# A gated-linear-attention stage on one Trainium2 core: decays computed during the projections, 64-token blocks, and the last pair's outputs placed inside the output projection

## What is computed

```python
y_f = _fourier_mix(z_f)                      # 256 of the 1024 output features
logg = log_sigmoid(z_g @ gate_w + gate_b) / 16
b = cumsum(logg, within a chunk)
qd, kd = q * exp(b), k * exp(-b)
att = where(mask, qd @ kd^T, 0)              # mask: lower triangle, 64 x 64
o = qd @ s + att @ v                         # s: 64 x 128 state before the chunk
s = s * exp(b_last) + (k * exp(b_last - b))^T @ v
o = o_forward + flip(o_backward)
y_g = rmsnorm(o over 128) * gla_norm * silu(z_r)
mix = concat(y_f, y_g) @ mix_w_out           # 1024 x 1024
```

## Time and profile before

| | us |
|---|---|
| median of 3 runs | 2854.75 (2853.38 to 2856.09) |
| the profiled execution | 2853.26 |
| its span in the trace | 2851.5 |
| TensorE matmul busy | 2745.1 (96%) |
| VectorE / ScalarE / GpSimd busy | 1292.9 (45%) / 1023.8 (36%) / 173.3 (6%) |
| chain that ended last | TensorE 89%, VectorE 6%, ScalarE 4% |
| mean granted clock of TensorE | 0.98 of full |

### The profile page before, as it was taken

How to read it: one execution, slowest core, us unless ns; L and a number is a source line. 1 busy time by engine, 2 the same in 40 slices (tenths; PEclk the granted TensorE clock), 3 DMA queues, 4 the chain that set the end, 5 groups by cost and what they waited for, 6 DMA issues and landing times.

```text
span 2851.5 us, 41295 instructions
## 1 busy us (share of the span) xinstructions
PE 2745.1 (96%) x18134; PEld 2420.4 (85%) x18134; DVE 1292.9 (45%) x1659; ACT 1023.8 (36%) x1291; POOL 173.3 (6%) x165
## 2 busy tenths in 40 slices
PE   7999999979999999999999889999999999988998
PEld 5877878767887787877888789999999999978998
DVE  4333334374423335332345655565555544554554
ACT  4222223332321223222233444443644444444443
POOL 0000010001000000000011000010010010133100
PEclk9999999979999999999999999999999999999999
DMA  7444344501444245444234135464445456653452
GB/s 272 145 148 151 104 156 140 185 15 61 146 163 158 96 142 177 137 148 156 77 112 133 45 105 177 161 208 154 154 142 174 158 174 186 190 130 103 134 197 84
DMA packets 398611, 406.18 MB, mean 142 GB/s; under 512 B 7264, under 2 KB 397104, under 8 KB 398432
## 3 DMA queue, kind: packets, MB, share of 16 engines
...
## 4 chain that ended last, share of the span: by engine, by line
PE 89%; DVE 6%; ACT 4%; issue 1%; DMA 0%; POOL 0%; SPq 0%; ACTq 0%; DVEq 0%; POOLq 0%
PE bank L96 88%; DVE w_lo L107 2%; ACT w_hi L103 1%; PE bank L99 1%; DVE tmp L115 1%; ACT x_hi L103 1%; DVE gla_att L107 1%; DVE gla_st L115 0%; DVE df_sc L124 0%; DVE x_lo L115 0%; ACT df_e L104 0%; ACT L103 0%; DMA ident<-in_ident 0%; POOL acc L107 0%; DVE gla_ls L118 0%
## 5 line engine op out<-in xcount | busy, mean ns | idle before, releaser
L107 DVE TENSOR_TENSOR w_lo<-w_raw,w_hi 128x2048 fp32r<-128x2048 f32 (+2 forms) x331 | 694.5, 2101 | 909.6 <-ACT w_hi L103 909.0
L96 PE MATMUL bank<-x_hi,w_hi 128*128 128x256 f32 (+1 forms) x3128 | 1031.0, 330 | 17.7 <-DVE w_lo L107 6.9
L96 PE MATMUL bank<-x_hi,w_lo 128*128 128x256 f32 (+1 forms) x3128 | 1021.2, 327 | 0.0
L96 PE MATMUL bank<-x_lo,w_hi 128*128 128x256 f32 (+1 forms) x3128 | 1016.2, 327 | 0.0
L103 ACT ACTIVATE w_hi<-w_raw 128x2048 fp32r<-128x2048 f32 (+2 forms) x331 | 578.4, 1750 | 462.9 <-PE bank L96 295.4
L96 PEld LDWEIGHTS bank<-x_hi,w_hi 128*128 128x128 f32 x3128 | 596.9, 191 | 81.5 <-issue 29.8
L96 PEld LDWEIGHTS bank<-x_hi,w_lo 128*128 128x128 f32 x3128 | 596.8, 191 | 50.1
L96 PEld LDWEIGHTS bank<-x_lo,w_hi 128*128 128x128 f32 x3128 | 594.9, 191 | 49.9 <-issue 0.7
L96 PE MATMUL bank<-hid_hi,w_hi 128*128 128x512 f32 (+1 forms) x1056 | 356.0, 337 | 1.7 <-ACT ada_rows L103 1.7
L96 PE MATMUL bank<-hid_lo,w_hi 128*128 128x512 f32 (+1 forms) x1056 | 354.9, 336 | 0.0
L96 PE MATMUL bank<-hid_hi,w_lo 128*128 128x512 f32 (+1 forms) x1056 | 354.8, 336 | 0.0
...
## 6 DMA issues: line engine op xcount, KB each, us to landing
...
```

Source lines behind the costliest of these rows:

```text
L96: return Issued(self.eng and self.eng.matmul(out, lhsT, rhs, start=start, stop=stop, skip_group_check=loose))
L107: return Issued(self.eng and self.eng.tensor_tensor(out, a, b, op))
```

## The change

Seven things change in the even mixer.

1. All decays are computed during the projections. `pe_gates` of pairs 0, 1 and 2 follow the rows units at 0, 1024 and 1280. VectorE puts their passes between the copies of the units at 1024, 1280 and 1536, ScalarE the exponentials and logarithms beside them; q, k and the results of all three pairs have places of their own, and r's places serve as scratch until SiLU fills them. The mask of the cumulative sum is loaded earlier, into the tile `diag`.
2. The products inside a block are 64 x 64 for each chunk, and the mask passes go over half as many elements.
3. The outputs come by token (128 tokens x 128 features): stationary are the masked products and the decayed queries, moving are v and the states. TensorE waits for its own inside part before it adds the part of the states.
4. The mean square is then a sum along the free axis: four activations with an accumulated sum for each head on ScalarE, a square root, a reciprocal and one multiplication on VectorE. The 24 matmuls of squares and the 24 of diagonals go; four transposes for each head (`pe_pair_turn`) turn the normed outputs into features by token.
5. Pair 0's inside work stands ahead of the Fourier mix, whose evictions move to ScalarE; its sums stay in PSUM until they are split.
6. In time, outputs of pair m follow the inside work of pair m+1.
7. The outputs and the turn of pair 2 stand inside `project_first` of the output projection, ahead of input blocks 4 and 6 (`aside`).

TensorE's side, SyncE's, ScalarE's and VectorE's (`pe_pair_turn` does four transposes for each head; `dve_gates`, `dve_decays` and `dve_decayed` keep their passes and change their places):

```diff
     for kk in range(1, KC):
+        if kk in aside:
+            aside[kk](e)
         wait_operand(e, x, kk)
         for i in range(4):
...
-    e.dma_start(Even(k).seg[:, :], k.io["segments"]).then_inc(k.load("seg"), "seg")
+    e.dma_start(t.seg, k.io["segments"]).then_inc(k.load("seg"), "seg")
 
...
     e.wait_ge(k.product, ("even", 2304, 1))
     e.dma_start(t.ft[:, :, :], k.io["fourier_time"]).then_inc(k.load("four_t"), "four_t")
+    e.dma_start(t.lim[:, :, :, :], k.io["limits"]).then_inc(k.load("lim"), "lim")
     e.dma_start(t.fd[:, :, :], k.io["fourier_dim"]).then_inc(k.load("four_d"), "four_d")
-    e.dma_start(t.lim[:, :, :, :], k.io["limits"]).then_inc(k.load("lim"), "lim")
...
     u.last = "even_g"
-    for c0, dst in ((0, "zf"), (1024, "v"), (1280, "v"), (1536, "v")):
+    for i, c0 in enumerate(EVEN_ROWS):
         u = take(e, ("even", c0), w, 0, KC, c0, 256)
         for tb in range(4):
-            bank = e.bank(("even", c0, tb), k.vector, (dst, c0, tb))
+            bank = e.bank(("even", c0, tb), k.vector, ("rows", c0, tb))
             project_rows(e, u, x, tb, bank).then_inc(k.product, ("even", c0, tb))
         u.last = ("even", c0, 3)
+        if i < 3:
+            pe_gates(e, t, i)
         pe_ada_step(e)
-    k.after(2, sp_even_segments)
-    pe_gates(e, t, 0)
     for c in range(3):
         u = take(e, ("even", 1792 + 256 * c), w, 0, KC, 1792 + 256 * c, 256)
...
+    pe_pair_inside(e, t, 0)
+    pe_fourier(e, t)
+    pe_pair_inside(e, t, 1)
+    pe_pair_outputs(e, t, 0)
+    pe_pair_inside(e, t, 2)
+    pe_pair_turn(e, t, 0)
+    pe_pair_outputs(e, t, 1)
+    pe_pair_turn(e, t, 1)
```

```diff
+    for d in range(2):
+        e.wait_ge(k.pooled, ("kd", m, d))
+        e.wait_ge(k.vector, ("qd", m, d))
+        banks = [e.bank(("inside", m, d, hl), k.vector, ("min", m, d, hl)) for hl in range(2)]
+        for tb in range(4):
+            for hl, par in ((0, 0), (1, 1), (0, 1), (1, 0)):
+                hs, ts = slice(64 * hl, 64 * hl + 64), slice((2 * tb + par) * 64, (2 * tb + par + 1) * 64)
+                mm = e.matmul(banks[hl][64 * par:64 * par + 64, tb * 64:(tb + 1) * 64],
+                              t.kd[hs, m, d, ts], t.qd[hs, m, d, ts], True, True)
+                if tb == 3 and (hl, par) in ((0, 1), (1, 0)):
...
+def pe_pair_outputs(e, t, m):
+
+    k = e.k
+    banks = [e.bank(("gla", 2 * m + hl), k.vector, ("normed", "gla", 2 * m + hl)) for hl in range(2)]
+    for d in range(2):
+        e.wait_ge(k.vector, ("max", m, d))
+        for tb in range(4):
+            for hl, par in ((0, 0), (1, 1), (1, 0), (0, 1)):
+                ps = slice(64 * par, 64 * par + 64)
+                mm = e.matmul(banks[hl][ps, tb * P:(tb + 1) * P], t.att[ps, m % 2, d, (4 * hl + tb) * 64:(4 * hl + tb + 1) * 64],
+                              t.v[ps, tb, (2 * m + hl) * P:(2 * m + hl + 1) * P], d == 0 and tb == 0, False, loose=True)
+                if d == 1 and tb == 3 and (hl, par) in ((1, 0), (0, 1)):
+                    mm.then_inc(k.product, ("gla_inside", 2 * m + hl))
     for hl in range(2):
-        hd = 2 * m + hl
-        for d in range(2):
-            e.wait_ge(k.vector, ("max", m, d, hl))
-            for tb in range(4):
-                e.matmul(banks[hl][:, tb * P:(tb + 1) * P], t.v[:, tb, hd * P:(hd + 1) * P], t.att[:, 2 * d + hl, tb, :],
-                         d == 0 and tb == 0, False, loose=True)
-    if m:
-        pe_gla_squares(e, 2 * m - 1, stat)
+        e.wait_ge(k.product, ("gla_inside", 2 * m + hl))
     for d in range(2):
         e.wait_ge(k.vector, ("state", m, d, 6))
         for s, c in enumerate(t.order[d][1:]):
+            ps, tb = slice(64 * (c % 2), 64 * (c % 2) + 64), c // 2
             for hl in range(2):
                 hs = slice(64 * hl, 64 * hl + 64)
-                mm = e.matmul(banks[hl][:, c * 64:(c + 1) * 64], t.st[d][hs, s, :], t.qd[d, m % 2][hs, c * 64:(c + 1) * 64],
-                              False, d == 1 and s == 6, loose=True)
+                mm = e.matmul(banks[hl][ps, tb * P:(tb + 1) * P], t.qd[hs, m, d, c * 64:(c + 1) * 64],
+                              t.st[hs, 2 * (m % 2) + d, s, :], False, d == 1 and s >= 5, loose=True)
                 if d == 1 and s == 6:
                     mm.then_inc(k.product, ("gla", 2 * m + hl))
-    pe_gla_squares(e, 2 * m, stat)
-
...
+
+    t = Even(e.k)
+    pe_mix_out(e, ("mix", 0), e.k.io["mix_w_out"][0], t.out, 2 * T, pe_ada_step,
+               {4: lambda e: pe_pair_outputs(e, t, 2), 6: lambda e: pe_pair_turn(e, t, 2)})
 
```

```diff
+    for i, c0 in enumerate(EVEN_ROWS):
         act_split(e, ("even", c0))
+        if i >= 2:
+            act_decays(e, t, i - 2)
+        if i:
+            act_gates(e, t, i - 1)
         act_ada_step(e)
-    act_gates(e, t, 0)
     for c in range(3):
         act_split(e, ("even", 1792 + 256 * c))
+        if c == 0:
+            act_decays(e, t, 2)
...
-    e.wait_ge(k.product, ("even", 2304, 1))
-    act_decays(e, t, 0)
+    act_keys(e, t, 0)
+    act_fourier(e, t)
+    act_keys(e, t, 1)
+    act_spreads(e, t, 0)
+    act_keys(e, t, 2)
+    act_high(e, t, 0)
+    act_spreads(e, t, 1)
+    act_high(e, t, 1)
+    act_spreads(e, t, 2)
+    act_high(e, t, 2)
...
+def act_spreads(e, t, m):
+
+    k = e.k
+    for hd in (2 * m, 2 * m + 1):
+        e.wait_ge(k.product, ("gla", hd))
+        if hd:
+            e.wait_ge(k.scalar, ("gla_square", hd - 1, 3))
+        for tb in range(4):
+            ts = slice(tb * P, (tb + 1) * P)
+            e.activation(t.zg[:, ts], k.out_of(("gla", hd))[:, ts], ACT.Square, accum=k.rs[:, 4 * hd + tb:4 * hd + tb + 1]).then_inc(
+                k.scalar, ("gla_square", hd, tb))
+        e.wait_ge(k.scalar, ("gla_square", hd, 3))
+        e.activation(k.rs[:, 4 * hd:4 * hd + 4], k.rs[:, 4 * hd:4 * hd + 4], ACT.Sqrt, scale=1.0 / GLA_DV,
+                     bias=k.eps[:, 0:1]).then_inc(k.scalar, ("gla_std", hd))
+
```

```diff
-    for c0, dst, name in ((0, t.zf, "zf"), (1024, t.v, "v"), (1280, t.v, "v"), (1536, t.v, "v")):
+    for i, c0 in enumerate(EVEN_ROWS):
         dve_split(e, ("even", c0))
-        at = c0 - 1024 if c0 else 0
+        at = c0 - 1024
         for tb in range(4):
             e.wait_ge(k.product, ("even", c0, tb))
-            e.tensor_copy(dst[:, tb, at:at + 256], k.out_of(("even", c0, tb))[:, 0:256]).then_inc(k.vector, (name, c0, tb))
+            dst = t.v[:, tb, at:at + 256] if c0 else t.zf[:, tb, :]
+            e.tensor_copy(dst, k.out_of(("even", c0, tb))[:, 0:256]).then_inc(k.vector, ("rows", c0, tb))
+            if i and tb == 0:
+                dve_gates(e, t, i - 1)
+            if i and tb == 1:
+                dve_log_gates(e, t, i - 1)
+                dve_decays(e, t, i - 1)
+            if i >= 2 and tb == 2:
+                dve_decayed(e, t, i - 2)
         dve_ada_step(e)
-    dve_gates(e, t, 0)
...
         dve_split(e, ("even", 1792 + 256 * c))
+        if c == 0:
+            dve_decayed(e, t, 2)
         dve_ada_step(e)
...
+    dve_inside(e, t, 0)
     for c in range(2):
         e.wait_ge(k.scalar, (("mix", 0), "hi", c))
-        e.tensor_tensor(k.x.lo[:, c, :], t.fy[:, c, :], k.x.hi[:, c, :].bitcast(F32), ALU.subtract).then_inc(
+        e.wait_ge(k.product, ("four_t", 3))
+        e.tensor_tensor(t.out.lo[:, c, :], k.out_of(("four_d", c))[:, :], t.out.hi[:, c, :].bitcast(F32), ALU.subtract).then_inc(
             k.vector, (("mix", 0), "lo", c))
...
+    dve_inside(e, t, 1)
+    dve_normed(e, t, 0)
+    dve_inside(e, t, 2)
+    dve_gated_heads(e, t, 0)
+    dve_normed(e, t, 1)
+    dve_gated_heads(e, t, 1)
+    dve_normed(e, t, 2)
+    dve_gated_heads(e, t, 2)
...
+def dve_normed(e, t, m):
+    k = e.k
+    for hd in (2 * m, 2 * m + 1):
+        e.wait_ge(k.scalar, ("gla_std", hd))
+        e.reciprocal(k.rs2[:, 4 * hd:4 * hd + 4], k.rs[:, 4 * hd:4 * hd + 4]).then_inc(k.vector, ("gla_rstd", hd))
+    for hd in (2 * m, 2 * m + 1):
+        e.wait_ge(k.vector, ("gla_rstd", hd))
+        e.tensor_tensor(t.turned(hd).rearrange("p (a b) -> p a b", a=4),
+                        k.out_of(("gla", hd))[:, :].rearrange("p (a b) -> p a b", a=4),
+                        columns(k.rs2[:, 4 * hd:4 * hd + 4]).broadcast_to([P, 4, P]), ALU.mult).then_inc(
+                            k.vector, ("normed", "gla", hd))
+
+
+def dve_gated_heads(e, t, m):
+    k = e.k
+    for hd in (2 * m, 2 * m + 1):
+        e.wait_ge(k.product, ("gla_turn", hd))
+        e.wait_ge(k.scalar, ("silu_r", hd))
+        e.scalar_tensor_tensor(t.r[:, hd, :], k.out_of(("gla_turn", hd))[:, :], k.small("gla_norm"), t.r[:, hd, :],
+                               ALU.mult, ALU.mult).then_inc(k.vector, ("gla_y", hd))
+    for hd in (2 * m, 2 * m + 1):
+        e.wait_ge(k.scalar, (("mix", 0), "hi", 2 + hd))
+        e.tensor_tensor(t.out.lo[:, 2 + hd, :], t.r[:, hd, :], t.out.hi[:, 2 + hd, :].bitcast(F32), ALU.subtract).then_inc(
+            k.vector, (("mix", 0), "lo", 2 + hd))
 
```

395 lines of the change are left out of this document (174 added, 221 removed).

## The result

The changed kernel takes 2811.39 us (2810.49 to 2812.64, 4 runs) against 2854.35 (2853.38 to 2856.09, 4 runs) for the kernel before: a ratio of 0.9846 with a 95% interval of 0.9834 to 0.9858. The profiled executions took 2811.14 and 2853.26 us, 42.1 apart, where I had forecast 33.2. By the ratio the time is 2810.8, 0.2 us under the range that I gave (2811 to 2840), which the interval does not resolve. The direction and the place were right; the gain that I forecast was too small by a quarter.

The account below looks back on a forecast made before the run. TensorE bounds up to 560 us, then waits on VectorE and ScalarE. Of 126.2 us behind the projections, 9.2 added ahead and 83.8 left behind gave 33.2 gained: 2822 us, range 2811 to 2840.

Parts of the forecast that it names:

- Ahead of 560: Before the projections end: two more pairs of gates' matmuls, two bank waits and a clock loss add 9.2 us.
- The wait for bank 7: At the rows unit at 1536, TensorE waits 2.7 us until VectorE has taken pair 1's gates.
- The second wait: Ahead of 560, TensorE waits 1.2 us for bank 5, freed by VectorE's low part, copy and first gates' pass.
- 64-column form: Products inside a block: 64 x 64 records over 64 columns, taken at 0.036 us each, 2.3 us a pair.
- the floor of my bounds: 2811 us: no clock loss, no second bank wait, and four tiles at once in the masked products.
- Squares: ScalarE's squares behind the projections: eight a pair at 0.41 us each, 3.3 us a pair.
- The clock: TensorE's slower clock behind waits, ahead of and behind the projections' end, costs 5.2 us in all.
- A: Rival: small products do not run side by side; masked products cost 11 us more, time 2833; chance 0.2.
- B: Rival: the clock stays up because gaps are short and apart; time 2811 to 2815; chance 0.2.
- C: Rival: VectorE paces the units at 1536 to 2304 and TensorE stays at 1.2 GHz; 2872, slower; chance 0.03.
- D: Rival: gain lost otherwise, such as SyncE's late loads (up to 19 us); within 0.2% of before; chance 0.03.
- The 84 us: Sign of being right: 84 us from the fold to the ada products behind the output projection's first four tiles.

Follow-up runs that it names:

- u1: The changed kernel with pair 2's outputs and turn ahead of the output projection instead of inside it: 2810.44 us.
- u2: The changed kernel with every 64 x 64 product inside a block issued twice: 2815.18 us.
- e4: The changed kernel with odd heads' token halves exchanged in PSUM, so the masked products use all four 64 x 64 tiles: 2805.26 us.
- u4: The changed kernel with VectorE's low part of weights behind the gates' first passes in the rows units at 1024, 1280 and 1536: 2808.14 us.
- u5: The changed kernel with ScalarE's gates ahead of its high part of weights and VectorE's low part behind the decays, in the rows units: 2805.67 us.

## Why the prediction was right or wrong

**Ahead of 560**, right. Forecast 9.2 us, measured 8.7. The gates cost 3.8. The wait for bank 7 was 2.03 (2.7), for the chain of load, high part, low part, copy and pass that I had followed. The clock behind it cost 2.5 (1.5): 25 records in 5.47 us (516.88 to 522.35), at 0.12 each 3.0. The second wait (1.2) did not appear, since the slow records made TensorE late; in u1 it did, with 2.36, and the sum was the same. SyncE did wait 17.0 us for the prenorm's low part, and TensorE waited for no load ahead of the fold: that cost nothing, as put.

**The small products**, the step that failed: "No row has the 64-column form; it lies between 0.036 and 0.073, and I take 0.036". The 0.036 were those of states of 128 columns; with half as many columns the price halves, and u2 gives 0.015. Both ends of my bracket were forms of 128 columns, so its lower end, which the floor of my bounds rests on, was no floor. Each pair took 1.0 us for these, not 2.3: 2.6 us too many in pairs 0 and 1 (pair 2's lie in a wait). The 0.036 was too high for the states too: 1.02 us for 28 records holds the tail of the last one, which is paid once, while 56 records that stand before others of the same tiles start every 0.027 us (585.15 to 586.68). 56 states took 1.5 us and not 2.0, eight transposes 1.0 and not 1.2; the masked products (3.7) were right. By place, from start to start in the changed kernel's rows:

| | forecast | measured |
|---|---|---|
| inside 0, inside 1 | 11.0 | 7.4 |
| Fourier mix | 10.3 | 10.5 |
| outputs 0 | 6.0 | 5.5 |
| from there to pair 2's states | 5.8 | 5.7 |
| from there to the turn of pair 1 | 14.9 | 13.6 |
| turn 1 | 2.6 | 1.6 |
| blocks 0 to 3 | 12.4 | 11.9 |
| outputs 2, blocks 4 and 5, turn 2 with its wait | 14.8 | 14.0 |
| blocks 6 and 7 | 6.0 | 5.6 |
| all | 83.8 | 75.7 |

Of the 8.1 us, inside 0 and 1 are 3.6, of which the form of 64 columns is 2.6: the largest single term, and a third of the whole. The rest is spread over many small ones, nearly all on the same side.

**Squares.** I took 0.41 us each from another stage, where the program makes each wait for the one before (`diff_sq`); here, without that wait, they follow each other at 0.25. From the outputs of pair 0 to pair 2's states it made no difference (5.7 us, forecast 5.8), as the states want the banks of both heads and so both norms; ahead of the turn of pair 1 it gave 0.8 of the 1.3 in the table (squares and roots of pair 1 took 2.8 us, 607.66 to 610.49, and not 3.6).

**The clock** was forecast at 5.2 us, and came about as large: 2.5 ahead of the fold (1.5), 1.5 behind the states' wait (1.0: 3.25 us for 56 records instead of 1.71), 0.9 in blocks 0 to 3 (1.5) and some more in turn 1, nothing in blocks 6 and 7.

**Rivals.** A (small products not side by side): refuted, by the 3.66 us of both orders and by the 1.93 of e4. B (the clock stays up) gave the number that came, 2811, by luck: the clock fell behind three of the four waits and cost what the forecast had, while the terms that B shares with the forecast were too large. C (VectorE paces the units and TensorE stays slow): VectorE does set F, as u1 and u4 show, but the units after the wait ran at full clock by 522.4, and u5 took the cost away by order alone; its own terms give 2873, not 2872. D, SyncE's later loads: behind the fold VectorE stood 3.1 us for the limits and TensorE 0.22 behind it, and no engine stood for another load.

**What would show it** held in three of five points: the wait at 1536 (2.0 us for about 3), the masked products, the turn of pair 1 as the longest wait. The 84 us were 76, the 2.3 us were 1.0. Of the signs against it two came: the granted clock of 0.88 from 520 to 530, and squares at 2.2 us a pair instead of 3.3.
